# Output projection and two LayerNorms token tile by token tile in a one-core decoder layer

## The reference

```python
# after attention: oa (8 heads), ob (three dilations, merged), ga and gb are gate logits
mix = (sigmoid(ga) * (oa @ w_proj_a) + sigmoid(gb) * (ob @ w_proj_b)) @ w_out
x   = layer_norm(ALPHA * x + gate1 * mix, ln1_g, ln1_b)      # gate1 = mod[2], per token group
h   = normalize(x) * (1 + scale2) + shift2                   # mod[4], mod[3]
moe = hier_moe(h)          # top-1 of 4 groups, top-2 of 8 experts; 32 SwiGLU experts, 1024 x 512
x   = layer_norm(ALPHA * x + gate2 * moe, ln2_g, ln2_b)
```

## Time and profile before

| | us |
|---|---|
| median of 3 runs | 1096.56 (1094.95 to 1098.03) |
| the profiled execution, its own time | 1094.32 |
| its span, first to last instruction | 1092.2 |
| PE busy | 847.7 (78%) |
| DVE busy | 344.8 (32%) |
| ACT busy | 182.7 (17%) |

### The profile page before, as it was taken

One profiled execution on the slowest core, in us unless ns is written; L12 is line 12 of the kernel. 1 busy time (PEld: TensorE's weight loads), 2 busy tenths in 40 slices (PEclk: granted clock), 3 DMA queues, 4 the chain that ended last, 5 costly groups with the idle time before them and its releaser, 6 DMA issues.

```text
span 1092.2 us, 11668 instructions
## 1 busy us (share of the span) xinstructions
PE 847.7 (78%) x4564; PEld 465.0 (43%) x4564; DVE 344.8 (32%) x520; ACT 182.7 (17%) x429; POOL 115.6 (11%) x116
## 2 busy tenths in 40 slices
PE   6599898989979999992618888777877777877840
PEld 5484676468864454871513323222222222322210
DVE  2048998793243321327411100000000000000018
ACT  2311223222221110003302111101011111111110
POOL 1212211110012112000010000000000000000020
PEclk9799999999998885996658999999999999999975
DMA  9986999587999999999983999999999999999931
GB/s 313 399 316 245 401 408 400 201 323 282 355 359 429 426 393 350 381 365 354 373 328 156 426 425 425 423 426 428 426 426 424 425 427 424 426 427 422 419 113 45
DMA packets 70084, 396.30 MB, mean 363 GB/s; under 512 B 6418, under 2 KB 13094, under 8 KB 47847
## 3 DMA queue, kind: packets, MB, share of 16 engines
q1 hardware_dynamic: 50928, 296.97, 68.2%
q0 software_dynamic: 12016, 85.90, 19.6%
q10 hardware_dynamic: 7104, 12.93, 3.4%
HBM read 387.89 MB, written 58.10 MB: 408 GB/s over the span
## 4 chain that ended last, share of the span: by engine, by line
PE 44%; DMA 37%; DVE 13%; issue 3%; ACT 1%; SPq 1%; ACTq 0%; POOL 0%; POOLq 0%; DVEq 0%
DMA ring<-in_w_exp_up_dram 28%; PE bank L801 12%; PE bank L436 10%; DVE ring L1220 3%; DMA ring<-in_cache_v_pages_dram,pidx 3%; DVE S L1224 3%; PE bank L716 3%; PE bank L446 3%; DMA ring<-in_w_in_dram 2%; PE bank L633 2%; PE bank L703 1%; DMA ring<-in_cache_k_pages_dram,pidx 1%; PE bank L819 1%; PE bank L523 1%; PE bank L462 1%
## 5 line engine op out<-in xcount | busy, mean ns | idle before, releaser
L801 PE MATMUL bank<-ring,hT 128*64 128x512 f32 x1024 | 243.6, 631 | 43.7 <-DMA ring<-in_w_exp_up_dram 41.2
L801 PEld LDWEIGHTS bank<-ring,hT 128*64 128x64 f32 x1024 | 89.7, 144 | 196.2 <-issue 196.2
L1601 DVE TENSOR_TENSOR hT<-hT,bank 128x256 f32<-128x256 f32 x32 | 19.3, 603 | 415.4 <-ACT hT L1144 415.4
L436 PE MATMUL bank<-hT,ring 128*128 128x264 f32 x576 | 140.9, 403 | 5.8 <-DMA ring<-in_w_in_dram 5.8
L819 PE MATMUL bank<-ring,hT 128*64 128x512 f32 x512 | 118.6, 604 | 19.5 <-DVE hT L1604 19.5
L436 PEld LDWEIGHTS bank<-hT,ring 128*128 128x128 f32 x576 | 112.1, 198 | 27.5 <-issue 7.8
L1220 DVE TENSOR_TENSOR ring<-ring,qbc 128x4096 f32<-128x4096 f32 x16 | 70.7, 4417 | 43.1 <-ACTq L846 41.2
L1743 POOL DMA_INDIRECT expert_rows<-work,ridx x32 | 31.1, 971 | 470.4 <-ACT work L838 351.4
L838 ACT ACTIVATE work<-bank 128x512 f32<-128x512 f32 (+5 forms) x83 | 36.6, 451 | 221.9 <-PE bank L819 145.2
L819 PEld LDWEIGHTS bank<-ring,hT 128*64 128x64 f32 x512 | 40.9, 138 | 76.6 <-issue 76.6
L1224 DVE TENSOR_REDUCE S<-ring 128x64 f32<-128x4096 f32 x16 | 70.6, 4414 | 0.3
(11 more groups left out here) (303 smaller groups left out, 783.1 us busy)
## 6 DMA issues: line engine op xcount, KB each, us to landing
ring<-in_w_exp_up_dram SPq DMA_DIRECT2D x32, 2048.0 KB, 22.0
ring<-in_w_exp_down_dram SPq DMA_DIRECT2D x32, 2048.0 KB, 21.8
ring<-in_w_exp_gate_dram SPq DMA_DIRECT2D x32, 2048.0 KB, 17.5
ring<-in_w_ada_dram SPq DMA_DIRECT2D x12, 2048.0 KB, 13.9
out_dram<-in_state_dil_kv_dram SPq DMA_DIRECT2D x6, 4064.0 KB
ring<-in_w_in_dram SPq DMA_DIRECT2D x11, 2048.0 KB, 21.1
out_dram<-in_state_dil_kv_dram ACTq DMA_DIRECT2D x16, 508.0 KB, 7.7
out_dram<-in_state_dil_kv_dram SPq DMA_DIRECT2D x8, 992.0 KB
```

Source lines behind the costliest of these rows:

```text
L436: i = mm(bk[:, 0:NT], w[:, k, j * P:(j + 1) * P], hT3[:, k, :], start=(k == 0), stop=(k == KC - 1))
L801: i = mm(side(2, half).rearrange("p (m n) -> p m n", m=2), xT[s][:, k, :], w[:, :, k, half * 256:(half + 1) * 256], start=(k == 0), stop=( ...
```

## The change

The output projection is computed token-major, one token tile after the other, in the order 2, 0, 1, and everything up to the router follows tile by tile while PE multiplies the next tile.

- For tiles 0 and 1 the tokens are the stationary operand and `w_out` the moving one: 2 halves of 512 channels, 8 contraction chunks each. For tile 2 the 8 tokens are stationary, and four blocks of 128 output channels go to partitions 0, 32, 64 and 96 of a bank; ACT copies them to a row (`mix8`).
- The gate now varies along the row. PE spreads the prompt's `gate1` over the partitions ahead of the softmax sums (ACT copies it to `g1p`), and turns the sample's just before the projection (`g1s`). The transposes of `mixT` go.
- DVE does, for each tile, gate, residual, the first LayerNorm and the second. ACT takes a root for each tile and norm (six in place of two).
- Turning, router product and turning back are done for each tile; the stream on PE is written below. ACT copies `g2p` and `g2s` after the six roots.

```diff
+            for h in range(2):                      # PE, ahead of the softmax sums
+                bk = take(("g1", h), 2 + h)
+                for j in range(4):
+                    i = mm(bk[:, j * P:(j + 1) * P], mod[:, 16 + 4 * h + j, NB:NB + 1].to_broadcast([P, P]), ident,
+                           start=True, stop=True)
+                done(("g1", h), i)
...
-            for j in range(KC):
-                half = ("wo", j // 4)
-                w = landed(pe, half).rearrange("p (k n) -> p k n", k=KC)
-                bk = take(("mix", j), j % 2)
+            for h in range(2):
+                bk = take(("g1s", h), 6 + h)
+                for j in range(4):
+                    i = tr(bk[0:NB, j * P:(j + 1) * P], mod[:, 16 + 4 * h + j, 0:NB], ident)
+                done(("g1s", h), i)
+            def mix_rows(t):
+                t0, tn = TT[t]
+                for h in range(2):
+                    landed(pe, ("wo", h))
+                    bk = take(("mix", t, h), 2 * (t == 0) + h)
+                    for k in range(KC):
+                        if t < 2:
+                            i = mm(bk[:, :], hT3[:, k, t0:t0 + tn], wo[h][:, k, :], start=(k == 0), stop=(k == KC - 1))
+                            continue
+                        for j in range(4):
+                            i = mm(bk[32 * j:32 * j + NB, 0:P], hT3[:, k, t0:t0 + tn], wo[h][:, k, j * P:(j + 1) * P],
+                                   start=(k == 0), stop=(k == KC - 1))
+                    done(("mix", t, h), i)
+                    last_use["wo", h] = ("mix", t, h)
...
+            mix_rows(2)
+            mix_rows(0)
+            turn_rows(2, 1)
+            mix_rows(1)
+            turn_rows(0, 2)
             for h in range(2):
                 bk = take(("g2", h), 6)
...
                 bk = take(("g2s", h), 7)
...
+            lgb = take("lg", 2)
+            pe.wait_ge(s_h2Ts, 1)
+            route(lgb, 2)
+            turn_back(2)
+            pe.wait_ge(s_h2T, 1)
+            route(lgb, 0)
+            turn_back(0)
+            turn_rows(1, 3)
+            pe.wait_ge(s_h2T, 2)
+            done("lg", route(lgb, 1))
+            turn_back(1)
...
+            root_of(2, 2)                           # ACT; root_of(n, t): wait for the n-th variance, of tile t
+            root_of(3, 2)
+            root_of(4, 0)
+            root_of(5, 0)
+            turned_rows(0, 0)
+            root_of(6, 1)
+            turned_rows(0, 1)
+            root_of(7, 1)
             for h in range(2):
                 bk = filled(act, ("g2", h))
...
+            turned_back(2)
+            turned_back(0)
+            turned_rows(1, 0)
+            turned_rows(1, 1)
+            turned_back(1)
...
+            for nth, t in enumerate((2, 0, 1)):     # DVE
...
+                    if t == 2:
+                        dve.wait_ge(s_mix8, h + 1)
+                        link(V.tensor_tensor(m, mix8[:, c], g1s[:, c], ALU.mult))
+                    else:
+                        bk = filled(dve, ("mix", t, h))
+                        freed(("mix", t, h), V.tensor_tensor(m, bk[:, :], g1p[:, c], ALU.mult))
...
+                    link(V.scalar_tensor_tensor(xt[:, c], xt[:, c], ALPHA, m, ALU.mult, ALU.add))
+                rows_norm(xt, t, tn)
+                link(V.scalar_tensor_tensor(xt, xt, nst[0:tn, t, 0:1], lng[0:tn, :], ALU.subtract, ALU.mult))
+                link(V.scalar_tensor_tensor(xt, xt, sdev[0:tn, t:t + 1], lnb[0:tn, :], ALU.mult, ALU.add))
+                rows_norm(xt, t, tn)
+                V.tensor_scalar(h2[0:tn, t, :], xt, nst[0:tn, t, 0:1], sdev[0:tn, t:t + 1], ALU.subtract, ALU.mult).then_inc(s_n2, 1)
```

More of the change, by code:

```diff
@@ L715, in _, with turn_rows, route @@
+            def turn_rows(t, nth):
+                t0, tn = TT[t]
+                pe.wait_ge(s_n2, nth)
+                for h in range(2):
+                    bk = take(("nT", t, h), 4 + h)
+                    for j in range(4):
+                        k = 4 * h + j
+                        i = tr(bk[:, j * P:j * P + tn], h2[0:tn, t, k * P:(k + 1) * P], ident[0:tn, 0:tn])
+                    done(("nT", t, h), i)
+            def route(bk, t):
+                t0, tn = TT[t]
                 for k in range(KC):
-                    i = mm(bk[:, 0:NT], w[:, k, (j % 4) * P:(j % 4 + 1) * P], hT3[:, k, :],
+                    i = mm(bk[0:tn, t * 36:(t + 1) * 36], hT3[:, k, t0:t0 + tn], wr[:, k, :],
@@ L717, in _, with turn_back @@
                            start=(k == 0), stop=(k == KC - 1))
[L718 to L721, removed]
+                return i
+            def turn_back(t):
+                t0, tn = TT[t]
                 for h in range(2):
-                    bk = take(("mt", t, h), 2 + h)
+                    bk = take(("h2", t, h), h)
                     for j in range(4):
-                        i = tr(bk[0:tn, j * P:(j + 1) * P], mixT[:, 4 * h + j, t0:t0 + tn], ident)
-                    done(("mt", t, h), i)
+                        i = tr(bk[0:tn, j * P:(j + 1) * P], hT3[:, 4 * h + j, t0:t0 + tn], ident)
+                    done(("h2", t, h), i)
@@ L1064, in _ @@
             A(own[:, 40:60], own[:, 40:60], ACT.Exp).then_inc(s_exp, 1)
+            for h in range(2):
+                bk = filled(act, ("g1", h))
+                freed(("g1", h), copy(g1p[:, h * 512:(h + 1) * 512], bk[:, :]), s_g1)
             act.wait_ge(s_rs, 1)
@@ L1148, in _ @@
                     copy(yrow[u], bank[4][:, :]).then_inc(s_yrow, 1)
-            root(4)
+            root(8)
             act.wait_ge(s_st, 16 * (3 * NB - EARLY + 3))
@@ L1465, in _ @@
-            V.memset(work[:, 0:512], 0.0).then_inc(s_h2T, 1)
+                    m = work[0:tn, 1024 + h * 512:1536 + h * 512]
+                    if t == 2:
[4 more added lines that the diff above has]
+                        freed(("mix", t, h), V.tensor_tensor(m, bk[:, :], g1p[:, c], ALU.mult))
+                        dve.wait_ge(free[turn["mix", t, h][0]], turn["mix", t, h][1] + 1)
@@ new lines, in _ @@
+                if t != 0:
+                    continue
+                for h in range(2):
+                    bk = filled(dve, ("nT", 2, h))
+                    hv = hT3[:, 4 * h:4 * h + 4, SEQ:NT]
+                    i = V.tensor_tensor(hv, bk[:, :].rearrange("p (k n) -> p k n", k=4)[:, :, 0:NB],
+                                        mod[:, 32 + 4 * h:36 + 4 * h, 0:NB], ALU.mult)
+                    freed(("nT", 2, h), i)
+                    dve.wait_ge(free[4 + h], turn[("nT", 2, h)][1] + 1)
+                    i = V.tensor_tensor(hv, hv, mod[:, 24 + 4 * h:28 + 4 * h, 0:NB], ALU.add)
+                    if h == 0:
+                        link(i)
+                    else:
+                        i.then_inc(s_h2Ts, 1)
@@ L1468, in _ @@
+            link(V.memset(work[:, 0:512], 0.0))
             lg = work[:, 112:220].rearrange("p (t n) -> p t n", t=3)
[L1469 removed]
             dve.wait_ge(s_rb, 32)
```

110 lines of the change are left out of this document (45 added, 65 removed).

## The result

The changed kernel takes **1087.6 us** (median of 4 runs, 1086.76 to 1089.29) beside 1097.3 of the kernel before (4 runs): ratio 0.9914, 95% interval 0.9895 to 0.9932. Measured once more beside other experiments it was 1087.59 against 1098.74: 0.9901, 0.9879 to 0.9923. So it is 9 to 11 us faster; the forecast was 1085.5, with 11.0 us.

A forecast was written before the change was run, and what follows sets the result against it. Bound: the serial chain to the first expert load, ahead of a DMA-full loop. Logits 11.4 us earlier, less 0.4 for lists, gain 11.0: 1083.3 against the profiled 1094.32, 1085.5 on medians; range 1078.5 to 1092.

The forecast's parts named there:

- The bound: Expert loop waits for weights with DMA full; starting its loads earlier moves the whole rest, until the hole is closed.
- the hole: Stretch before the expert loop, 571 to 589 us, where the DMA engines stand still; the only thing to gain.
- The cap of 18.0 us: Most that earlier expert loads can gain: the hole without DMA, 589.05 - 571.
- The projection: Output projection from 457.2 to 491.3 us: gate turns 1.0, tile 2 3.9, two tiles 14.1 each, turning 1.0.
- the 8-token tile: Tile 2's product in the projection, four column blocks: 3.9 us if they overlap, 14.1 if not.
- The last tile's rows: DVE's residual, statistics and affine steps after the projection: 8.5 us, last root released at 499.8.
- The queue behind the last root: ACT's expert-gate copies behind the last root hold PE and its router products: 18.7 us, logits read at 518.5.
- rival B: Clock is up after the last root or rises during the turns: 13 to 19 us, capped at 18.0; chance 0.20.
- scattered and read back with the copies running: Token lists between logits and first expert load: 0.4 us charged, cutting the gain from 11.4 to 11.0.
- Rival D: Lists crawl behind the window copies, scatter alone costing 23.4 us more; about 1108 us, chance 0.06.
- Rival E: SP's later release lets its queue run dry: 11 us at worst, gain 7; chance 0.13 with smaller losses.
- the edits at nothing: Spreading the prompt's gate in PE's idle before the softmax sums (2.0 us, 4.0 at worst), later SP loads: no cost.

The follow-up runs named there:

- e1: The changed kernel with ACT's copies of the expert gate and its copy back of tile 2 moved ahead of the last root; 1085.08 us, ratio 0.9902 to before.
- e6: The changed kernel with the last 14 window copies in runs of 16384 bytes instead of 4096; 1100.37 us, ratio 1.0012 to the kernel before.
- e9: e1 with two loads of the first expert pair (down weights, gate weights) cut into 4 KB runs; 1077.36 us, ratio 0.9799 to the kernel before.
- e2: The changed kernel with the 8-token tile multiplied in one column block instead of four side by side; 1097.0 us, ratio 1.0007 to the kernel before.
- e4: The changed kernel with 8 unread matmuls in PE's idle time between the expert gate's two halves; 1087.38 us, ratio 0.9915 to the kernel before.
- e8: e1 with the four earlier window copies and the last 14 in 2 KB runs; 1084.24 us, ratio 0.9853 to the kernel before.
- e10: As e9, but with those two loads and the last 14 window copies in 2 KB runs; 1078.31 us, ratio 0.981 to the kernel before.
- e7: The changed kernel with the four earlier window copies in 4 KB runs instead of 16 KB; 1091.02 us, ratio 0.9925 to the kernel before.
- e5: e1 with the four earlier window copies in 4 KB runs instead of 16 KB; 1085.36 us, ratio 0.9874 to the kernel before.

## Why the prediction was right, point by point

**The bound.** Right. From the first load to the end of the span the kernel before takes 503.2 us, the changed one 503.7, e1 503.6, e6 503.6 (e9, with the hole nearly closed, 504.4): the loop moves as a block, and the time is set by when that load is issued, until the hole is closed. The cap of 18.0 us was a little low. e9 issues the load 20.2 us sooner than the kernel before, since ahead of the hole there was slack too: while the list was read back alone, after 567 us, the engines were at 64%.

**The projection.** Forecast 34.1 us from its start to its end, measured 33.1 (461.02 to 494.12). The 3.9 us for the 8-token tile was 3.68; e2 shows that the other end of that bound, 14.1, would have eaten the gain. **The last tile's rows**: 8.5 forecast, 8.4 measured (494.12 to 502.52).

**The queue behind the last root.** 18.7 forecast, 18.05 measured, and the mechanism was the one named: PE idle 6.95 us, released by ACT's gate copy. It was at half clock only in part. The changed kernel's stretches:

```profile
499.60:509.20 9.60, 5.93 (x39) 4.57 (x39) 4.21 (x8) 3.42 (x6) 2.14 (x4) 0.50 1.05 351
509.20:516.60 7.40, 3.54 (x31) 3.30 (x30) 0.00 (x0) 6.00 (x12) 0.00 (x0) 0.96 0.92 305
516.60:520.50 3.90, 3.69 (x18) 3.70 (x19) 0.00 (x0) 0.11 (x1) 0.00 (x0) 0.50 1.00 300
```

Between 509.2 and 516.6 the clock was full, so that two of the turns took 1.07 and 1.04 instead of 2.0, and tile 0's router product 2.12, where the last tile's took 3.63. For the last router product, after 4.07 us without work, it was half: 3.63 us, where 16 such products took 1.87 in e1 at full clock. So of rival B only a small part happened. I had weighed the page "TensorE: Matmul & The Clock Gate" of the Trainium skill, Part 4, which has transposes not bring in the full clock; by it the last product would be at half. It was, but no run here shows that as the transposes' doing: in e1 and e4 too the product came after an idle of 3 to 4 us.

**The lists: the term that was mis-sized.** I charged 0.4 us for "scattered and read back with the copies running", because both took 10.43 and 8.17 "nearly all under full DMA engines". For reading back that was a wrong reading: the copies gave out halfway through it. The forecast let them end at 571 us in both kernels; their last packet came at 567.6 us in the kernel before and at 575.0 in the changed one, 110.4 and 114.0 us after the projection's start. From the logits to the first load it became 63.15 us instead of 59.14, 4.0 more and not 0.4. With the 1.8 us by which the path up to the logits was shorter than forecast, 11.0 + 1.8 - 3.6 = 9.2, which is what the load shows. The time came out 2.1 us over the forecast, 0.7 of it because the kernel before was measured at 1097.3 and not at 1096.56. That it came so near is in part luck: two errors of opposite sign, 1.8 and 3.6 us, lie in it.

**Rival D, the lists that crawl.** It got 6 in 100 and didn't happen, but its mechanism was there. I had set against it a rule of the Trainium skill ("DMA: Bandwidth & Descriptors", section "Queues, rings and completion order"): an engine takes its queues in turn, packet by packet. The trace agrees with the rule, 285 packets against 285, but for the stretch of e8 shown above. My conclusion from it, that a list then doesn't suffer from the copies, was wrong. Taking turns by packet makes a small packet's queue depend on the size of the others' packets: 25.5 us for the scatter opposite 12.6 KB (e6), 16.8 opposite 12.3 (e1, where these gave out at 542 us and 4 KB followed), 10 opposite 3.9 (e9), 7.4 opposite 2.0 to 2.2 (e10). The changed kernel was spared D because its last copies were in 4 KB runs and the two loads had passed; e6 has the same kernel without that, and no gain.

**Rival E and the edits at nothing.** SP's queue did not run dry: the weights issued at 487.28 and 494.15 landed 48.8 and 47.1 us later, the 14 issues took 58.76. The spreading of the prompt's gate took 1.95 us of PE's idle ahead of the softmax sums, as costed; 4.32 us of that idle are left.

**Open.** Why the projection starts 3.8 us later in the profiled execution of the changed kernel than in that of before. 1.7 us of it are there at 300 us already (ACT's copy at 301.94 instead of 300.21), ahead of every edit. From the softmax sums to the projection it is 134.9 us against 132.8, and in the other kernels, all with the change, between 132.2 and 136.6. So I take no part of it as the change's, but no run separates it. Open are also the stretch of e8, and e10 with SP's first load of the loop ahead of the last copies, for which it now waits.

## What to carry to other kernels

When a small transfer is on the critical path and bulk copies run beside it, look at the packet counts per queue in that stretch: where they are equal, the bulk's packet size is the small transfer's price, and cutting only those pieces of the bulk that lie opposite gives it back. A step that is moved earlier meets other neighbours; price it by what lies in the queues at its new time, and read from the trace how much of the old duration really had company. And ask what stands behind an added wait on every engine's queue: here two copies behind a root held another engine's ready work for 7 us.

## What the runs showed that I had not expected

Starting the lists sooner did not make them end sooner: issued at 81.6, 78.8 and 73.3 us after the projection's start, the scatter landed at 92.0, 91.9 and 90.0. Packet for packet, the share of a queue went from 25% (12.3 KB opposite) over 50% (3.7 KB) to 65% (2.0 KB). And cutting 10 MB of copies from 16 KB to 4 KB runs cost SP 53.01 us of writing instead of 17.10, yet no time that could be told from noise (e7). The two loads queued behind them were issued 27 to 30 us later, and their packets still met the scatter as before (e5).
